# One VectorE instruction that adds the mask, scales and keeps the row extreme, in the softmax of both attentions

## The reference

```
# layer 2, "att": 8 heads of 128; S = 256 makes one block, so this is plain causal attention
q, k = rotary(rms_norm(q, q_gain)), rotary(rms_norm(k, k_gain))
s = where(k_pos <= q_pos, einsum('bhqd,bhkd->bhqk', q, k) * 128 ** -0.5, -inf)
out = softmax(s) @ v

# layer 3, "dsa": 8 heads over one latent of 128; each query keeps the 64 keys of best score
_, idx = lax.top_k(where(allowed, score, -inf), 64)
logits = einsum('bqhc,bqkc->bqhk', q_abs, kv_sel) * 64 ** -0.5
p = softmax(where(valid, logits, -inf)); ctx = p @ kv_sel
```

## Time and profile before

| | |
|---|---|
| median of 3 runs | 1441.23 us (1439.14 to 1444.85) |
| span of the profiled execution, first to last instruction | 1440.5 us |
| its PE busy | 1208.6 us (84%) |
| its DVE busy | 602.0 us (42%) |
| its ACT busy | 436.6 us (30%) |
| first attention, first scores to last evacuation | 557.13 to 579.07 us |
| second attention, the same | 915.24 to 938.59 us |
| experts' weights stream | from 944.21 us to nearly the end |

### The profile page before, as it was taken

How to read it: one execution, slowest core, us unless ns; L and a number is a source line. 1 busy time by engine, 2 the same in 40 slices (tenths; PEclk the granted TensorE clock), 3 DMA queues, 4 the chain that set the end, 5 groups by cost and what they waited for, 6 DMA issues and landing times.

```text
span 1440.5 us, 19204 instructions
## 1 busy us (share of the span) xinstructions
PE 1208.6 (84%) x8218; PEld 876.4 (61%) x8218; DVE 602.0 (42%) x967; ACT 436.6 (30%) x688; POOL 16.2 (1%) x32
## 2 busy tenths in 40 slices
PE   5999989999999997999999999897564665635677
PEld 5998766699887786599988676654221321312222
DVE  4678414577444677277643558822100100101001
ACT  4653320444333675254333513532010000000001
POOL 3000000000000000000000000000000000000000
PEclk9999999999999999999999999998886878868889
DMA  8352669455555553245554723079999999999994
GB/s 265 131 188 106 215 210 338 150 191 193 177 178 193 195 186 117 87 164 191 198 180 153 239 91 118 1 318 408 429 428 428 428 429 427 429 429 428 429 427 189
DMA packets 98352, 363.04 MB, mean 252 GB/s; under 512 B 7225, under 2 KB 10644, under 8 KB 86372
## 3 DMA queue, kind: packets, MB, share of 16 engines
q1 hardware_dynamic: 96240, 357.70, 64.0%
q0 software_dynamic: 1680, 4.10, 1.0%
q10 hardware_dynamic: 356, 0.13, 0.0%
HBM read 360.87 MB, written 1.05 MB: 251 GB/s over the span
## 4 chain that ended last, share of the span: by engine, by line
PE 60%; DMA 21%; DVE 7%; ACT 2%; issue 2%; SPq 1%; DVEq 0%; ACTq 0%
PE bank L917 33%; DMA arena<-in_exp_w 21%; PE bank L625 7%; PE bank L1031 3%; PE bank L1559 2%; DVE arena L2218 2%; PE bank L889 2%; PE bank L1224 2%; PE bank L702 2%; PE bank L856 1%; PE bank L899 1%; SPq L2811 1%; PE bank L1241 1%; PE bank L1255 1%; DVE arena L2141 1%
## 5 line engine op out<-in xcount | busy, mean ns | idle before, releaser
L625 PE MATMUL bank<-arena 128*32 128x512 f32 x880 | 187.4, 695 | 78.1 <-DMA arena<-in_exp_w 77.1
L1722 DVE TENSOR_TENSOR low_w<-ring,split_high 128x2048 fp32r<-128x2048 f32 x84 | 189.6, 2288 | 104.1 <-ACT split_high L2412 104.0
L917 PE MATMUL bank<-turned_high,low_w 128*128 128x256 f32 x720 | 204.6, 284 | 0.0
L2412 ACT ACTIVATE split_high<-ring 128x2048 fp32r<-128x2048 f32 x84 | 157.7, 1916 | 137.0 <-DMA ring<-in_w_down 67.6
L625 PE MATMUL bank<-ring,arena 128*32 128x512 f32 x528 | 93.5, 691 | 79.6 <-DMA arena<-in_exp_w 79.6
L917 PE MATMUL bank<-turned_high,split_high 128*128 128x256 f32 x512 | 145.9, 285 | 3.0 <-DVE turned_low L1737 3.0
L917 PE MATMUL bank<-turned_low,split_high 128*128 128x256 f32 x512 | 144.9, 283 | 0.0
L917 PEld LDWEIGHTS bank<-turned_high,low_w 128*128 128x128 f32 x720 | 139.2, 193 | 0.0
L625 PEld LDWEIGHTS bank<-arena 128*32 128x32 f32 x880 | 49.1, 125 | 140.2 <-issue 140.2
L771 DVE TENSOR_TENSOR arena<-arena,bank 128x512 f32<-128x512 f32 x8 | 5.5, 687 | 295.6 <-PE bank L625 253.3
L625 PEld LDWEIGHTS bank<-ring,arena 128*32 128x32 f32 x528 | 26.8, 125 | 142.8 <-issue 142.8
(11 more groups left out here) (450 smaller groups left out, 1948.7 us busy)
## 6 DMA issues: line engine op xcount, KB each, us to landing
arena<-in_exp_w SPq DMA_DIRECT2D x59, 2048.0 KB, 23.0
ring<-in_exp_w SPq DMA_DIRECT2D x33, 2048.0 KB, 20.3
ring<-in_w_up SPq DMA_DIRECT2D x16, 2048.0 KB, 9.0
ring<-in_w_down SPq DMA_DIRECT2D x16, 2048.0 KB, 7.8
ring<-in_mod_w SPq DMA_DIRECT2D x12, 2048.0 KB, 8.8
ring<-in_w_in_ar SPq DMA_DIRECT2D x7, 2048.0 KB, 8.3
ring<-in_w_qkv SPq DMA_DIRECT2D x6, 2048.0 KB, 8.1
ring<-in_ple_gate SPq DMA_DIRECT2D x4, 2048.0 KB, 8.5
```

Source lines behind the costliest of these rows:

```text
L625: last = nc.tensor.matmul(mb[bank][strip(e), :], act[:, k, strip(e)], w[e][:, k, cols], start=(k == 0), stop=(k == n_k - 1), skip_group_ch ...
L917: last = mm(dst, *pair, start=(start and i == 0), stop=(stop and i == 2))
L1722: v.tensor_tensor(low_of(name, s), half_of(slot(name), name, s), high_of(name, s).bitcast(F32), ALU.subtract).then_inc(sem("split_low"), 1)
L2412: nc.scalar.activation(high_of(name, s), half_of(slot(name), name, s), ACT.Copy)\
```

## The change

In both attentions the scaled sum and the row maximum become one VectorE call, `tensor_tensor_reduce`. It computes `part = (scores + mask) * by`, where `by` is now the negated scale, and keeps the running minimum of `part`, started from `LARGE`, in `nmax[:, i]`. Because the sign is turned, that minimum is the negated maximum of the scaled row, as before, and ACT's exponential gets `scale=-1.0`. The call also signals the bank's `freed` semaphore, and ACT waits for that one in place of the semaphore of the row maximum, which goes. The masks are now multiplied by the scale too; at 0 and -1e30 that changes nothing in the result. `q_root` is negated once by one more small instruction before "att", with a wait in front of it. The call is built as two instructions, the second of which writes only the 128x1 result. Line numbers on DVE move by one or two, since `LARGE` adds a line ahead and lines go away in `attend`.

```diff
-            def attend(tag, scale, mask, probs, extra=None):
+            def attend(tag, minus_scale, mask, probs):
@@
-                        by = scale(i // 2, t) if callable(scale) else scale
-                        v.scalar_tensor_tensor(part, bank.ap[:, 0:(t + 1) * P], by, mask(t), ALU.mult, ALU.add)\
-                            .then_inc(bank.freed, 1)
-                        banks.wait_read(dve, tag, "s", i)
-                        v.tensor_reduce(nmax[:, i:i + 1], part, AX.X, ALU.max, negate=True).then_inc(sem(tag + "_max"), 1)
+                        by = minus_scale(i // 2, t) if callable(minus_scale) else minus_scale
+                        v.tensor_tensor_reduce(part, bank.ap[:, 0:(t + 1) * P], mask(t), by, LARGE, ALU.add, ALU.min,
+                                               nmax[:, i:i + 1]).then_inc(bank.freed, 1)
@@
-            v.reciprocal(q_root, q_root)
+            step(v.reciprocal(q_root, q_root))
+            v.tensor_scalar(q_root, q_root, -1.0, None, ALU.mult)
             step(v.reciprocal(k_root, k_root))
@@
-            attend("dsa", 64.0 ** -0.5, lambda t: bias2[:, t, 0:(t + 1) * P], prob2)
+            attend("dsa", -(64.0 ** -0.5), lambda t: bias2[:, t, 0:(t + 1) * P], prob2)
@@ on ScalarE
-                        act.wait_ge(sem(tag + "_max"), i + 1)
-                        s.activation(part, part, ACT.Exp, bias=nmax[:, i:i + 1], accum_out=rsum[:, i:i + 1])\
+                        banks.wait_read(act, tag, "s", i)
+                        s.activation(part, part, ACT.Exp, bias=nmax[:, i:i + 1], scale=-1.0, accum_out=rsum[:, i:i + 1])\
```

More of the change, by code:

```diff
@@ L34 @@
 NEG = -1e30
+LARGE = 3e38
 TAPS = 31
```

## The result

The changed kernel takes 1428.67 us (median of 6 runs, 1426.89 to 1435.45) against 1441.37 us (6 runs): a ratio of 0.992, 95% interval 0.9902 to 0.9937, a gain of 11.5 us (9.1 to 14.1); the two medians are 12.7 us apart. The profiled execution has a span of 1426.8 us in place of 1440.5.

A forecast was written before the change was run, and what follows sets the result against it. VectorE was taken to set both attentions' pace, ahead of the experts' weight stream. Savings of 3.8 us in "att" and 3.9 in "dsa", together 7.7, less 0.2 for contact, gave 1441.2 - 7.5 = 1433.7 us; range 1430.5 to 1441.

The forecast's parts named there:

- the bound: VectorE sets the pace in both attentions; the experts' weight stream behind them waits for a release, so it starts earlier.
- the road: The stretch behind "att", nearly all dense products, with one 7.99 us transfer that moves along: no gain lost there.
- The rival that only "dsa" pays: Something between the attentions keeps its own time, so only the second one's 3.9 us count: 1437 us, chance 0.07.
- my own signs of being wrong: Among them: the first experts' load comes earlier by much more or less than the two attention stages have shrunk.
- The new main instruction: In both attentions, it takes what the scaled sum took: 346 and 477 ns in "att", 285 and 420 in "dsa".
- like the scan: Rival: the running minimum in both attentions streams slowly, costing 5.4 of 7.7 us; gain 2.3 us, 1439, chance 0.20.
- at a fixed 0.5 us: Rival: each new call in both attentions has its own fixed price; at 0.5 us, 8.3 us slower, 1449.5, chance 0.08.
- The second instruction and what lies between: In both attentions, the accumulator read takes 0.15 us, less one overlap of 0.09: 0.48 us saved for an "att" pair.
- My best end: A second instruction of 0.06 us in both attentions: 0.66 us saved for a pair, 10.6 us for 16 pairs.
- The rival that the second half is nearly free: The call's second instruction costs almost nothing in both attentions: a gain of 10 us, 1431 us, chance 0.15.
- What is late next: ScalarE's 15.34 us in "att" and TensorE's 17.98 in "dsa" cap savings at 6.6 and 5.4 us; 0.2 off for contact.
- The Trainium skill's rule that fusing is not worth it, since the number of operations counts: In both attentions, only the row maximum's streaming would go: 0.41 us for a pair, 6.6 us for 16.

The follow-up runs named there:

- att_only: The kernel before with the new call in the first attention alone, the second keeping the old pair of instructions: 1436.76 us, 0.9958 of before.
- read_waited: The changed kernel with one more VectorE wait, behind the new call, for its accumulator read to end: 1434.78 us, 0.9951 of before.
- The delays: The changed kernel with VectorE memsets ahead of one attention's first item: with five memsets 0.998 and 0.9974 of before, with one 0.994, 0.9942 and 0.9949.

## Why the prediction was wrong

*The sign, the bound and the road* were right. VectorE did set the pace in both stages, the gain reached the end of the program through an earlier start of the stream, and nothing of the first attention's gain was lost on the way: 4.7 us at its end, and the dense stretch behind it no longer than before (253.85 for 254.17). The rival that only "dsa" pays is out: att_only gained 6.1 us. One of my own signs of being wrong did show: the load came 13.0 us earlier, the stages had shrunk by 9.3.

*The new main instruction* was right to a few nanoseconds. The rivals that priced it, like the scan or at a fixed 0.5 us, are out.

*The second instruction and what lies between* is the step that failed. I counted one overlap of 0.09 and then 0.15 us for the read, so 0.41 and 0.54 us for the two widths. Measured are 0.27 and 0.40: the read is 0.08 long and lies wholly under the start of the next instruction. That is 0.76 us saved for a pair in place of 0.48, in both attentions. My best end had the read at 0.06 us on the path, so even that end was too high: I bounded the length of the read and never asked whether it takes a place in the row at all. ScalarE's own accumulator read, in the trace before, does overlap with its ACTIVATE, and did not teach me the rest. The rival that the second half is nearly free, to which I gave 0.15, is the one that came true; it named 10 us. read_waited shows what the hiding is worth: 2.1 us over both stages.

*What is late next* was named rightly and sized too gently. The floors of 6.6 and 5.4 us held, and TensorE and ScalarE took over. The floor of "dsa" was softer than I wrote: TensorE's 17.98 us were measured with the clock at 0.90, and at full clock the same products kept it busy for 15.68. Eight pairs at 0.75 would be 6 us, and 4.7 and 4.6 arrive; the 0.2 us that I took off for contact over both stages should have been 1.3 for each. The two errors go against each other: 7.5 forecast for the stages, 9.3 measured, of which some 0.4 in "dsa" is the clock.

*The Trainium skill's rule that fusing is not worth it, since the number of operations counts* ("VectorE: DVE Perf Modes", "Rules for kernel authors"), gave 6.6 us. The stages gave 9.3. The rule does not fit here: the count stayed at four for an item, but one of the four became free.

*What I had not in the sum at all* is 2 to 3 us beyond the stages. In the traces it is TensorE's clock ahead of "dsa" (81.7 to 78.9 us with the same instructions). The delays show that other builds with the same instructions there lose it again; that the changed kernel has it in most of its executions is luck and not the change. With 7.5 us forecast and this step, the total would still have been at the edge of the range; with 9.3 alone it would have been inside, at 1432. By the read alone the range would have held; by the read and the clock together it failed. Two things stay open: why one program keeps its pattern over most executions while an edit of 0.3 us far behind alters it, and how the earlier part of the program (the start of "att" moves by 4.6 us between traces) takes part in it.

## What to carry to other kernels

A VectorE instruction with an accumulator output costs here (float32, 128 and 256 columns, a running minimum) what the plain instruction costs, as long as nothing waits on VectorE itself for the result; so a reduction behind an element-wise step can go for nothing. Ask of a new small instruction not only how long it is but whether it takes a place on the path. And a gain below 0.5% in a program like this one is to be read by the stages of its traces, since the clock can add or take as much as the change itself.

## What the runs showed of the hardware

- The custom form with a running minimum takes 281 and 425 ns for 128 and 256 columns from PSUM with a constant scale, 345 and 485 with one per partition; the read of the accumulator takes 84 ns and starts about 0.07 us before the main instruction's end, together with the next instruction, if that has no wait for it.
- A VectorE instruction with no wait in front started 0.07 to 0.09 us before the end of the one ahead of it. With a wait for the accumulator read, the reciprocal started 0.12 us after the read's start, and without the wait 0.00 (read_waited, changed).
- TensorE's clock fell to half although the engine is shown as busy (before: 14.73 of 15 us, at 0.77, during products of 36 columns behind products of 2). The same products ran at 1.00 in the three traces of the changed kernel. The stretch ahead of "dsa" took 78.9 us plus half of its time at half clock in all traces.
- The stream of the experts' weights is 453.3 to 456.2 us long if the first experts' products start within 41.4 us of its beginning, and 458.0 to 458.3 in five of six traces in which they started after 44.6 us or later.
